# Paired products on halves of the array, split scan tiles and other thirds of mem's products in a four-layer kernel on one core

## What is computed

```
x = first_block(x):     layer 0: even_mixer, then conv_ffn; layer 1: odd_mixer, then conv_ffn
                        each followed by layer_norm(ALPHA * x + .)
x = second_block(x):    layer 2: window attention + cross attention on mem, then conv_ffn_2
                        layer 3: hgrn2 (gated scans) + cross attention on mem, then conv_ffn_2

even_mixer:  idx   = einsum('bthd,bsd->bths', q_idx, k_idx)        # 8 index heads of 64
             score = einsum('bth,bths->bts', w_idx, relu(idx)); top 64 keys of each query
             oa    = softmax(q_lat c^T + bias, chosen keys) c, then einsum('bshr,hrd->bshd', oa, w_uv)
             ob    = softmax(q_b k_b^T + gates, causal) v_b        # 8 heads of 64
window:      16 heads of 64 over 4 key heads, keys within 128, softmax with a sink, times v
cross:       4 heads of 128 over 256 rows of mem; mem_kv = rmsnorm(mem) @ w_mem_kv[layer]
hgrn2:       8 heads; q * sigmoid(q), gates f = lb + (1 - lb) * sigmoid(z), both directions;
             out = sum over keys of (q, decayed k) * v, normed and gated
```

## Time and profile before

| what | us |
|---|---|
| median of the runs | 1436.08 |
| profiled execution, its own time | 1435.02 |
| its span, first to last instruction | 1433.7 |
| layer 0 up to its first norm | 0 to 168 |
| norm 0 | 168 to 178 |
| norm 2 | 463 to 472 |
| norm 3 | 660 to 677 |
| window stage, loop | 706 to 787 |
| scan stage, loop | 1070 to 1205 |

### The profile page before, as it was taken

One profiled execution on the slowest core, in us unless ns is written; L12 is line 12 of the kernel. 1 busy time (PEld: TensorE's weight loads), 2 busy tenths in 40 slices (PEclk: granted clock), 3 DMA queues, 4 the chain that ended last, 5 costly groups with the idle time before them and its releaser, 6 DMA issues.

```text
span 1433.7 us, 23122 instructions
## 1 busy us (share of the span) xinstructions
PE 1392.6 (97%) x9591; PEld 1251.8 (87%) x9591; DVE 937.8 (65%) x1511; ACT 727.5 (51%) x1063; POOL 221.6 (15%) x186
## 2 busy tenths in 40 slices
PE   7999999999999999999899999999999999899998
PEld 6887799999888899997777899999689988799997
DVE  4875476667785766676566266556566888665555
ACT  4654264555442654453555364455457766544543
POOL 4570300000000000001732600000222334000000
PEclk8999999999999999999999999999999999899999
DMA  7622175555462556542512355654344344355551
GB/s 276 217 97 118 60 263 177 221 192 179 183 233 89 206 182 228 183 176 104 185 60 89 118 217 195 210 200 178 136 171 162 120 141 184 118 203 195 197 184 59
DMA packets 36698, 240.40 MB, mean 168 GB/s; under 512 B 3889, under 2 KB 6257, under 8 KB 9202
## 3 DMA queue, kind: packets, MB, share of 16 engines
q1 hardware_dynamic: 36594, 238.92, 45.8%
HBM read 236.27 MB, written 2.64 MB: 167 GB/s over the span
## 4 chain that ended last, share of the span: by engine, by line
PE 82%; DVE 9%; ACT 4%; issue 3%; DMA 1%; POOL 1%; ACTq 0%; SPq 0%; DVEq 0%
PE ps L398 23%; PE ps L361 16%; PE ps L362 16%; PE ps L363 16%; PE ps L528 1%; ACT whi L290 1%; DVE ar L2167 1%; PE ps L533 1%; PE ps L855 1%; PE ps L1675 1%; DVE wlo L312 1%; DMA raw<-in_up 1%; PE ps L509 1%; PE ps L1941 1%; PE ps L1573 1%
## 5 line engine op out<-in xcount | busy, mean ns | idle before, releaser
L361 PE MATMUL ps<-XS,whi 128*128 128x256 f32 x2088 | 599.6, 287 | 3.5 <-DVE wlo L307 2.9
L362 PE MATMUL ps<-XS,whi 128*128 128x256 f32 x2088 | 595.2, 285 | 0.0
L363 PE MATMUL ps<-XS,wlo 128*128 128x256 f32 x2088 | 594.9, 285 | 0.0
L312 DVE TENSOR_TENSOR wlo<-raw,whi 128x2048 fp32r<-128x2048 f32 x163 | 372.5, 2287 | 127.3 <-ACT whi L290 127.3
L290 ACT ACTIVATE whi<-raw 128x2048 fp32r<-128x2048 f32 x203 | 387.0, 1907 | 131.5 <-PE ps L398 80.4
L361 PEld LDWEIGHTS ps<-XS,whi 128*128 128x128 f32 x2088 | 405.2, 194 | 9.3 <-issue 4.4
L362 PEld LDWEIGHTS ps<-XS,whi 128*128 128x128 f32 x2088 | 405.1, 194 | 2.1 <-issue 0.5
L363 PEld LDWEIGHTS ps<-XS,wlo 128*128 128x128 f32 x2088 | 405.2, 194 | 0.0
L398 PE MATMUL ps<-whi,MS 128*128 128x512 f32 x1024 | 290.5, 391 | 0.0
L298 POOL TENSOR_TENSOR wlo<-raw,whi 128x512 fp32r<-128x512 f32 x158 | 204.7, 1331 | 288.3 <-ACT whi L290 204.7
L398 PEld LDWEIGHTS ps<-whi,MS 128*128 128x128 f32 x1024 | 189.7, 188 | 37.6 <-issue 0.4
(11 more groups left out here) (286 smaller groups left out, 1332.1 us busy)
## 6 DMA issues: line engine op xcount, KB each, us to landing
raw<-in_up SPq DMA_DIRECT2D x88, 1024.0 KB, 4.8
raw<-in_down SPq DMA_DIRECT2D x44, 1024.0 KB, 4.8
raw<-in_hg_t SPq DMA_DIRECT2D x16, 1024.0 KB, 4.8
raw<-in_od_t SPq DMA_DIRECT2D x8, 1024.0 KB, 4.9
raw<-in_ev_a SPq DMA_DIRECT2D x6, 1024.0 KB, 10.1
raw<-in_wa_o SPq DMA_DIRECT2D x6, 1024.0 KB, 4.8
raw<-in_hg_o SPq DMA_DIRECT2D x6, 1024.0 KB, 4.7
raw<-in_ev_o SPq DMA_DIRECT2D x4, 1024.0 KB, 6.2
```

Of the source, the lines that this page charges most:

```text
L312: ve.tensor_tensor(lo[:, 0:w], r[:, 0:w], hi[:, 0:w].bitcast(F32), ALU.subtract).then_inc(w_lo_v)
L361: pe.matmul(d, hi[:, c], S[:, k, 0:256], start=(k == 0), stop=False)
L362: pe.matmul(d, hi[:, c], S[:, k, 256:512], start=False, stop=False)
L363: last = pe.matmul(d, lo[:, c], S[:, k, 0:256], start=False, stop=(k == 7))
```

## The change

Five edits. Index scores of heads h and h + 1 are issued in turns, row half by row half. The value products of two heads (own values in layer 0, and the window heads) are issued in the step of the second one, in turns on the two column halves; the post products likewise, one step after the second one's turn. In the scan stage the odd tiles `hg_t` are cut in two: GpSimd has columns 0 to 1023, VectorE the rest, and TensorE and SP wait for both. VectorE's part of the next `at_q` stands at the end of its step. `CUTS` has other portions for norms 0, 2 and 3, and the key product that now can come ahead of norm 3's first transposes waits until the bank that it writes has been read.

```diff
-CUTS = [[[(0, 0, 8)], [(0, 8, 9)], [(0, 9, 16)]],
+CUTS = [[[(0, 0, 8)], [(0, 8, 13)], [(0, 13, 16)]],
         [[(0, 0, 8)], [(0, 8, 16)], []],
-        [[(0, 0, 4)], [(0, 4, 5)], [(0, 5, 8)]],
-        [[(0, 0, 8)], [(1, 0, 5)], [(1, 5, 16)]],
+        [[(0, 0, 4)], [(0, 4, 6)], [(0, 6, 8)]],
+        [[(0, 0, 8), (1, 0, 6)], [(1, 6, 12)], [(1, 12, 16)]],
...
+SHARED = [_t[0] == "hg_t" and _t[1] % 2 == 1 for _t in SCHED]
-LOV = np.cumsum([not _p and _m in PLACE for _m, _p in enumerate(POOLT)]).tolist()
+LOV = np.cumsum([(not _p or SHARED[_m]) and _m in PLACE for _m, _p in enumerate(POOLT)]).tolist()
...
-                elif POOLT[o]:
-                    sp.wait_ge(w_lo_p, LOP[o])
                 else:
-                    sp.wait_ge(w_lo_v, LOV[o])
+                    if POOLT[o]:
+                        sp.wait_ge(w_lo_p, LOP[o])
+                    if not POOLT[o] or SHARED[o]:
+                        sp.wait_ge(w_lo_v, LOV[o])
...
-                for a in range(0, w, 512):
+                for a in range(0, w // 2 if SHARED[m] else w, 512):
...
-            if m in PLACE and not POOLT[m]:
+            if m in PLACE and (not POOLT[m] or SHARED[m]):
...
-                ve.tensor_tensor(lo[:, 0:w], r[:, 0:w], hi[:, 0:w].bitcast(F32), ALU.subtract).then_inc(w_lo_v)
+                c = slice(w // 2 if SHARED[m] else 0, w)
+                ve.tensor_tensor(lo[:, c], r[:, c], hi[:, c].bitcast(F32), ALU.subtract).then_inc(w_lo_v)
...
-            else:
+            if not POOLT[m] or SHARED[m]:
                 pe.wait_ge(w_lo_v, LOV[m])
...
+                if n == 3 and name == "mem_k":
+
+                    pe.wait_ge(xr.sem, xr_at(3, 0, 0))
...
-            for h in range(8):
+            for h in range(0, 8, 2):
+
                 pe.wait_ge(e_ac.sem, 3 + h // 4)
                 if h >= 4:
-                    pe.wait_ge(e_re.sem, h - 3)
+                    pe.wait_ge(e_re.sem, h - 2)
...
-                    ins = pe.matmul(bank[h % 4][:, a:b], QI[q, c:c + 128], KI[q, 0:b - a], start=True, stop=True)
-                ins.then_inc(e_ix.up())
+                    for r in range(2):
+                        q = slice(64 * r, 64 * r + 64)
+                        ins = pe.matmul(bank[(h + r) % 4][:, a:b], QI[q, c:c + 128], KI[q, 0:b - a], start=True, stop=True)
+                        if tt == 1:
+                            ins.then_inc(e_ix.up())
...
-                if 0 <= i - 4 < 16:
+                if 0 <= i - 4 < 8 and i % 2:
+                    turned_pe(i - 5, 0)
                     turned_pe(i - 4, 0)
-                    value_b(i - 4) if i - 4 < 8 else value_a(i - 12)
-                if 0 <= i - 13 < 8:
-                    post_a(i - 13)
+                    values_b(i - 5)
+                if 8 <= i - 4 < 16:
+                    turned_pe(i - 4, 0)
+                    value_a(i - 12)
+                if 0 <= i - 13 < 8 and i % 2 == 0:
+                    posts_a(i - 14)
...
+            for r in range(2):
+                pe.matmul(o[64 * r:64 * r + 64, 0:256], VB[:, 64 * (h + r):64 * (h + r) + 64], ePT[r][:, 0:256], start=True, stop=False)
+            for r in range(2):
+                pe.matmul(o[64 * r:64 * r + 64, 128:256], VB[:, 512 + 64 * (h + r):576 + 64 * (h + r)], ePT[r][:, 256:384],
+                          start=False, stop=True).then_inc(a_va.up())
...
+            for r in range(2):
+                pe.wait_ge(e_oa.sem, h + r + 1)
+                pe.matmul(ePAIR[p % 2][64 * r:64 * r + 64, 0:256], WV[:, 64 * (h + r):64 * (h + r) + 64], OA[r], start=True,
+                          stop=True).then_inc(e_po.up())
...
-                if 0 <= i - 4 < 20:
+                if 0 <= i - 4 < 16 and i % 2:
+                    turned_pe(i - 5, WB)
                     turned_pe(i - 4, WB)
-                    window_value(i - 4) if i - 4 < 16 else cross_value(X0, i - 20, i - 4)
+                    window_values(i - 5)
+                if 16 <= i - 4 < 20:
+                    turned_pe(i - 4, WB)
+                    cross_value(X0, i - 20, i - 4)
...
             for s in range(2):
-                last = pe.matmul(o[q, 0:256], VN[:, 256 * s + 64 * kvh:256 * s + 64 * kvh + 64],
-                                 wPT[i % 2][:, 256 * s:256 * s + 256], start=(s == 0), stop=(s == 1))
-            last.then_inc(a_va.up())
+                for r in range(2):
+                    kvh = 2 * (c // 4) + r
+                    last = pe.matmul(o[64 * r:64 * r + 64, 0:256], VN[:, 256 * s + 64 * kvh:256 * s + 64 * kvh + 64],
+                                     wPT[r][:, 256 * s:256 * s + 256], start=(s == 0), stop=(s == 1))
+                    if s == 1:
+                        last.then_inc(a_va.up())
...
             copy_dve(3, HB, xT, hPT, 512)
+            dve_weights(at_q(1))
             cross_split_dve(2)
...
                     ms_low(n - 3, ON[(n - 3) % 2])
+                dve_weights(min(at_q(n + 1), LAST[6]))
             dve_weights(NEXT[6])
```

More of the change, by code:

```diff
@@ L967, in even_pe @@
             ins.then_inc(e_fw.up())
-            for h in range(8):
+            for h in range(0, 8, 2):
                 pe.wait_ge(e_ac.sem, 3 + h // 4)
                 if h >= 4:
-                    pe.wait_ge(e_re.sem, h - 3)
+                    pe.wait_ge(e_re.sem, h - 2)
                 else:
                     pe.wait_ge(m_ev.sem, 8)
-                q = slice(64 * (h % 2), 64 * (h % 2) + 64)
                 for tt in range(2):
@@ L1034, in pair_free, with values_b @@
                 pe.wait_ge(ms_lo.sem, E0 + p - 1)
-        def value_b(h):
-            if h % 2 == 0:
-                pair_free(h // 2)
+        def values_b(h):
+            pair_free(h // 2)
             pe.wait_ge(e_ac.sem, AT_VB)
             o = ePAIR[h // 2 % 2]
-            q = slice(64 * (h % 2), 64 * (h % 2) + 64)
-            v = slice(64 * h, 64 * h + 64)
-            pt = ePT[h % 2]
-            pe.matmul(o[q, 0:256], VB[:, v], pt[:, 0:256], start=True, stop=False)
-            pe.matmul(o[q, 128:256], VB[:, 512 + 64 * h:576 + 64 * h], pt[:, 256:384], start=False,
-                      stop=True).then_inc(a_va.up())
+            for r in range(2):
[3 more added lines that the diff above has]
+                          start=False, stop=True).then_inc(a_va.up())
         def latent_query(h):
@@ L1079, in value_a, with posts_a @@
             pe.matmul(bank[6][:, 128:256], CN[:, 128:256], pt[:, 256:384], start=False, stop=True).then_inc(a_va.up())
-        def post_a(h):
+        def posts_a(h):
             p = 4 + h // 2
-            if h % 2 == 0:
-                pair_free(p)
+            pair_free(p)
             if h == 0:
                 pe.wait_ge(d_wv, 16)
-            pe.wait_ge(e_oa.sem, h + 1)
-            q = slice(64 * (h % 2), 64 * (h % 2) + 64)
-            pe.matmul(ePAIR[p % 2][q, 0:256], WV[:, 64 * h:64 * h + 64], OA[h % 2], start=True, stop=True).then_inc(e_po.up())
+            for r in range(2):
+                pe.wait_ge(e_oa.sem, h + r + 1)
+                pe.matmul(ePAIR[p % 2][64 * r:64 * r + 64, 0:256], WV[:, 64 * (h + r):64 * (h + r) + 64], OA[r], start=True,
+                          stop=True).then_inc(e_po.up())
         def even_act():
@@ L1665, in window_score, with window_values @@
             return last
-        def window_value(i):
-            c, r, h = whead(i)
-            kvh = 2 * (c // 4) + r
+        def window_values(i):
+            c = i // 2
             o = wV[c % 2]
-            q = slice(64 * r, 64 * r + 64)
-            if r == 0 and c >= 2:
+            if c >= 2:
                 pe.wait_ge(ms_lo.sem, W0 + c - 1)
             for s in range(2):
-                last = pe.matmul(o[q, 0:256], VN[:, 256 * s + 64 * kvh:256 * s + 64 * kvh + 64],
-                                 wPT[i % 2][:, 256 * s:256 * s + 256], start=(s == 0), stop=(s == 1))
-            last.then_inc(a_va.up())
+                for r in range(2):
[4 more added lines that the diff above has]
+                        last.then_inc(a_va.up())
         def sink_of(i):
```

## The result

The changed kernel takes 1424.88 (median of four runs, 1424.04 to 1426.75) against 1436.8 before (median of four, 1435.43 to 1440.69): a ratio of 0.9915, with a 95% interval of 0.9892 to 0.9937. The profiled execution took 1424.84 (span 1423.5), which is 10.2 less than that of before. The forecast was 14.4 less in the profile and 1421.7 as a median; the time lies in its range, but the sum came out of terms of which only some were right.

The account below looks back on a forecast made before the run. TensorE, with 82% of the chain, was taken to bound the kernel. Terms 0 + 4.0 + 2.4 + 3.4 + 4.6 = 14.4 took the profiled 1435.02 to 1420.6, median 1421.7; range 1413 to 1430.

Parts of the forecast that it names:

- Index scores: Layer 0's index scores in pairs: row halves already interleave, so worth 0, between -0.4 and 0.3.
- Values and posts of layer 0: Pairs on column halves at one product's price: values 2.4, posts 2.1, less 0.5 for a waiting copy; 4.0.
- Norms 0 and 2: Moved thirds of mem's products fill TensorE's idle before the second transposes: 0.7 and 0.6.
- Norm 3: Six of mem's products moved before the first transposes fill TensorE's idle of 1.93 plus 0.25 of stretching: 2.1.
- a gain passes down between the stages: Between stages all is bound by TensorE or hangs on the previous stage's end, so no gain is lost there.
- rival 5: Anywhere: one more clock fall costs up to 3.4, one fewer gains as much; two or three more, chance 0.02.
- Window stage: Paired value products, limited by VectorE's idle; stretches 1 to 4 between projections 0.4, 1.7, 1.0, -0.7: 2.4.
- Rival 2: Window loop stays with TensorE, keeping 8 of 10.1 saved: 5.6 more, 1416.1; chance 0.08.
- Scan stage: Splitting tiles between GpSimd and VectorE shortens masked-add waits; long periods gain 0.78 each, 4.6 in all.
- Rival 1: Scan split gains nothing, VectorE's half taking back what shorter GpSimd work gives: 9.8 faster, 1426.3; chance 0.12.
- rival 4: Scan: VectorE's half waits a full piece each time and both adds still wait: 6.7 slower, 1442.8; chance 0.03.
- rival 3: Column halves don't overlap at 256 columns, a pair costing two products: 8.3 faster, 1427.8; chance 0.05.

Follow-up runs that it names:

- e7: The changed kernel with layer 0's post products issued one by one again, as before the change; 1426.07, ratio 0.99.
- e4: The kernel before with only layer 0's pairs added (index scores, own values and post products); 1437.08, ratio 0.9987.
- e5: The changed kernel with four places instead of two for the window stage's transposed weights; 1422.85, ratio 0.988.
- e9: The changed kernel with three quarters of GpSimd's low part of the window stage's first output tile left out; 1421.1, ratio 0.9883.
- e12: The changed kernel with four window places, single layer 0 posts, and keys copied out before the query tile's high part; 1422.88, ratio 0.9895.
- e10: The changed kernel with four places for the window stage's transposed weights and its value products one by one again; 1426.37, ratio 0.9916.
- e1: The kernel before with only the new thirds of mem's products (norms 0, 2 and 3) and their wait; 1434.09, ratio 0.9965.
- e3: The kernel before with only the window heads' value products in pairs; 1438.09, ratio 0.9996.
- e8: The changed kernel with VectorE taking the whole of each scan tile it shared with GpSimd; 1426.1, ratio 0.9905.
- e11: The changed kernel with four places for the window stage's transposed weights and single post products in layer 0; 1422.99, ratio 0.9889.

## Why the prediction was right or wrong

**Index scores**: 0 forecast, 0 measured.

**Values and posts of layer 0**: 4.0 forecast, 2.1 measured. The price of a pair was right, and so were the three pairs that count (2.3 against 2.4) and the first that gives nothing. The step that failed is the posts' tail: I took off 0.5 for one copy that waits. TensorE waited 0.39, 0.19 and 0.67 there, and e7 shows that the paired posts are the cause, since all three waits go with them. The posts were worth -0.2 (e7), not 1.6. As I read the kernel, with only two places for attention outputs both copies behind a pair wait for it, and VectorE's scalings come late behind them; more places there were not tried.

**Norms 0 and 2**: 0.7 and 0.6 forecast, 0.7 and 0.7 measured. That of norm 0 comes again in every trace with the new thirds; that of norm 2 is -0.2 to 1.0 there, so its agreement is in part luck. **Norm 3**: 2.1 forecast and 2.4 measured where it was forecast, but the sentence that a gain passes down between the stages failed right there. The rotation hung on the landing of the query tile, which starts when mem's tile is through: I read of the next 15 us only that the projection's inputs were ready. That chain starts earlier by the gain, so it would have kept it, had the tile not taken 1.2 longer; the other 1.6 are a fall of the clock. The prediction named that as rival 5, an edge of every case, and gave a chance, 0.02, only to two or three falls more. It wasn't a rare case: among the fourteen traces five have a fall that starts between 679.8 and 682.7; all of those have the new thirds, five more with them have none, and e4 has one at 668.8 with the old thirds.

**Window stage**: 2.4 forecast, 1.0 measured. Stretch 2 gave 1.63 (1.7 forecast). Stretch 4 came out at -0.2, where -0.7 was forecast; the copy behind the pair, on which that rested, is there and larger (e5: 1.4), and so is what the pairs save. Stretch 3 failed: 1.0 forecast, -0.2 measured. I counted VectorE's busy time as its work, though some of it was waiting for GpSimd, and I had held that only two-input instructions are held up. A scaling with one tensor, 0.62 for two, took 2.3 beside GpSimd (e9). The Trainium skill, SBUF — State Buffer, section on the two separate sides, names VectorE instructions in a two-port mode beside those with two inputs; e9 agrees with it as far as the wait goes, though no row shows the mode, and the prediction used only half of that sentence. Stretch 1 (0.4 forecast) lost 1.1, and here two causes stand side by side. The copy behind the pair is one: with four places e5 has 18.96. The clock is the other: the stretch is at half clock for 6.2 in the changed kernel, 5.3 in e5 and in e12 (19.02) and 3.1 before. With single products it takes 18.77, 18.83, 19.00, 19.13 and 19.29 at 3.1, 3.2, 3.7, 3.9 and 4.3 of half clock, so about 0.4 for each microsecond. By that (an estimate from these five traces, carried on beyond them) the 3.1 more of half clock cost the changed kernel about 1.3, which is all of the loss, and about 0.4 of e5's 0.9 is clock as well. The gain of 0.9 in the loop's first stretch was in no term: it is GpSimd's pieces out of the way of the rotary product, and e10, with single products, has it too (15.33), so it isn't the pairs'. Rival 2 (8 of the 10.1 kept) is out: even with four places the five stretches gain 3.6.

**Scan stage**: 4.6 forecast, 6.3 measured, the right mechanism and a wrong size. GpSimd's second piece ends 3.6 after the half begins, as forecast. The term that was mis-sized is the period. I took the ring of VectorE and GpSimd to set every long one, at about 15.1, with the masked product 1.8 behind the start of the half (1.1 and 0.7) and adds of about 1.9. It does so in the last two alone, where the product stands 1.80 behind and the adds take 1.75, and it needs 14.71. In the periods ahead of these the product stands 2.68, 2.34 and 2.06 behind the half, so that the adds meet less or nothing of GpSimd's second piece, and TensorE sets the pace. The four long periods lose 1.42, 1.40, 1.26 and 1.12 instead of 0.78 each. By these numbers a loop over more heads would go on at about 14.7, which no run shows. TensorE's own work was read wrongly, too: I took it from the last period, 14.15, which has 116 records where a full one has 165. It is 14.43, and so the first two periods gave 0.6 each instead of 0.8 and 0.7. Rival 1 (nothing gained) and rival 4 (slower) are out; rival 3 (halves in turn) is out by the pair's 0.80.

Together: terms too high by 1.9 in layer 0, 2.8 behind norm 3 and 1.4 in the window stage, one too low by 1.7 in the scan. The time lay in the range, partly because these errors cancel, and that is luck.

## What to carry to other kernels

Where two short products share the halves of the array, a pair costs what one did; before you count on it, look at what the delay of the first does to the buffers that its release frees. In the window stage the engines that refill them ran behind the pair until there were four places instead of two. Where GpSimd and VectorE work side by side, don't read VectorE's busy time as its work: set the shortest duration of each instruction against its mean. And when a gap is filled, read the next 20 us after it for the wait that hangs on the same event, and for instructions of VectorE that a shifted piece of GpSimd's will meet or miss. Before two traces are compared stretch by stretch, set beside each stretch how much of it was at half clock.

## What the runs showed of the hardware

TensorE's clock fell at other places from run to run: in layer 1 to 1.2 GHz for 3.4, 6.8, 10.2 or 13.7, in kernels that differ there in norm 2 at most. Windows of the same stretch, first of e1, then of the changed kernel:

```profile
418.00:438.00 20.00, 20.00 (x85) 14.52 (x84) 10.18 (x22) 3.85 (x6) 0.00 (x0) 0.66 0.35 131
```

```profile
418.00:438.00 20.00, 20.00 (x119) 16.42 (x118) 10.15 (x21) 5.07 (x8) 0.00 (x0) 0.83 0.25 97
```

These windows hold 85 records of TensorE at 0.66 and 119 at 0.83, though not quite the same products. A fall of 3.4 cost 1.5 where TensorE was busy (28.44 against 29.92 of e3, and 29.93 of e8 with a fall from 753.5 to 756.9), and 0.3 in the window loop's first stretch, where TensorE is busy for 11.4 of 15.3 and waits for the others in between (15.01 of e7, none of it at half clock, against 15.34 of the changed kernel, with 3.3). A longer wait ahead of it doesn't decide: e11 waited 2.78 ahead of the rotation without a fall, e9 2.04 with one. So a difference of 2 us between two kernels of this kind is told by their stretches, at equal clock, and not by their times.

The same load of 1 MB, the first of two issued 0.4 apart, landed after 4.7 to 6.6 in the fourteen traces, and with ScalarE's old order the wait at the rotation followed it one to one (4.71 and 1.55, 5.92 and 2.77, 6.60 and 3.46). Why it is mostly longer with the new thirds is open; nothing here tells it.
